# Value projections as pairs of chunks of 512 output columns by half the contraction

## The reference

```
layer 0:  x += 0.5 ffn(x);  x += pool_mixer(x) + memory_attention;  x += 0.5 ffn(x)
layer 1:  x += 0.5 ffn(x);  x += diff_attention(x) + memory_attention;  x += 0.5 ffn(x)
layer 2:  x += norm(moba(x), retention(x));  x += norm(cross_attention(x, mem));  x += norm(ffn(x))

memory values, layers 0 and 1:  v = mem_n @ mem_w_kv[:, 512:1024]       256 x 512
differential attention:         v = h @ w_in[:, 2048:3072]              256 x 1024, 8 heads of 128
layer 2:                        mv = h @ w_in[:, 1024:1536]             256 x 512, 8 heads of 64
                                rv = h @ w_in[:, 2048:2560]             256 x 512, 4 heads of 128
cross attention:                v = mem_n @ w_ckv[:, 1024:2048]         256 x 1024
```

## Time and profile before

| | |
|---|---|
| median of three executions | 1621.92 us |
| profiled execution, first to last instruction | 1619.9 us |
| matmuls busy | 1520.8 us, 94% |
| VectorE busy | 1033.5 us, 64% |
| ScalarE busy | 722.8 us, 45% |
| mean granted TensorE clock | 0.976 |
| weights and inputs read | 254.64 MB, 158 GB/s |

### The profile page before, as it was taken

One profiled execution on the slowest core, in us unless ns is written; L12 is line 12 of the kernel. 1 busy time (PEld: TensorE's weight loads), 2 busy tenths in 40 slices (PEclk: granted clock), 3 DMA queues, 4 the chain that ended last, 5 costly groups with the idle time before them and its releaser, 6 DMA issues.

```text
span 1619.9 us, 28718 instructions
## 1 busy us (share of the span) xinstructions
PE 1520.8 (94%) x12056; PEld 1483.4 (92%) x12056; DVE 1033.5 (64%) x1234; ACT 722.8 (45%) x905; POOL 1.9 (0%) x7
## 2 busy tenths in 40 slices
PE   5999998999999999999989999999898999799996
PEld 5999998999999999999977999999787898699996
DVE  5555588665455755568777864557857864764555
ACT  5443454454344544454445544445344443343442
POOL 0000000000000000000000000000000000000000
PEclk9999999999999999999989999999999899799998
DMA  6655553445555445544333345454334242245450
GB/s 240 222 179 186 182 182 104 157 147 180 193 177 179 165 180 181 187 177 172 114 105 118 143 160 204 167 180 173 118 117 156 88 173 105 104 141 198 173 181 35
DMA packets 35837, 256.84 MB, mean 159 GB/s; under 512 B 3984, under 2 KB 4112, under 8 KB 4912
## 3 DMA queue, kind: packets, MB, share of 16 engines
q1 hardware_dynamic: 35424, 253.48, 44.0%
q0 software_dynamic: 336, 2.23, 0.3%
HBM read 254.64 MB, written 1.05 MB: 158 GB/s over the span
## 4 chain that ended last, share of the span: by engine, by line
PE 80%; DVE 14%; ACT 4%; issue 1%; DMA 0%; SPq 0%; ACTq 0%; DVEq 0%
PE prod L791 16%; PE prod L792 16%; PE prod L793 16%; PE acc L791 8%; PE acc L793 8%; PE acc L792 8%; DVE four L1253 4%; DVE w_lo L1206 3%; ACT w_hi L1018 1%; DVE acts_l L1258 1%; PE prod L820 1%; PE prod L822 1%; PE prod L821 1%; PE aux L843 1%; PE acc L896 1%
## 5 line engine op out<-in xcount | busy, mean ns | idle before, releaser
L791 PE MATMUL prod<-acts_h,w_hi 128*128 128x256 f32 x2352 | 679.2, 289 | 35.7 <-DVE w_lo L1206 18.2
L792 PE MATMUL prod<-acts_l,w_hi 128*128 128x256 f32 x2352 | 672.3, 286 | 0.0
L793 PE MATMUL prod<-acts_h,w_lo 128*128 128x256 f32 x2352 | 671.9, 286 | 0.0
L1206 DVE TENSOR_TENSOR w_lo<-raw,w_hi 128x2048 fp32r<-128x2048 f32 x238 | 543.8, 2286 | 57.2 <-ACT w_hi L1018 57.0
L1018 ACT CAST w_hi<-raw 128x2048 fp32r<-128x2048 f32 x238 | 451.5, 1899 | 166.7 <-PE acc L793 102.8
L791 PEld LDWEIGHTS prod<-acts_h,w_hi 128*128 128x128 f32 x2352 | 458.1, 195 | 40.0 <-DVE w_lo L1206 18.2
L792 PEld LDWEIGHTS prod<-acts_l,w_hi 128*128 128x128 f32 x2352 | 458.1, 195 | 1.2 <-issue 1.0
L793 PEld LDWEIGHTS prod<-acts_h,w_lo 128*128 128x128 f32 x2352 | 457.7, 195 | 0.0
L791 PE MATMUL acc<-mix_h,w_hi 128*128 128x256 f32 x1200 | 343.2, 286 | 3.2 <-DVE mix_l L1524 2.2
L792 PE MATMUL acc<-mix_l,w_hi 128*128 128x256 f32 x1200 | 340.6, 284 | 0.0
L793 PE MATMUL acc<-mix_h,w_lo 128*128 128x256 f32 x1200 | 340.5, 284 | 0.0
(11 more groups left out here) (152 smaller groups left out, 961.8 us busy)
## 6 DMA issues: line engine op xcount, KB each, us to landing
raw<-in_weights_dram SPq DMA_DIRECT2D x238, 1024.0 KB, 4.8
mem_x<-in_mem_dram POOLq DMA_DIRECT2D x2, 1024.0 KB, 6.6
tabs<-in_tabs_dram SPq DMA_DIRECT2D x1, 1697.0 KB, 13.2
x_res<-in_x_dram SPq DMA_DIRECT2D x2, 512.0 KB, 6.3
out_dram<-x_res SPq DMA_DIRECT2D x4, 256.0 KB, 2.1
masked<-in_lambda_dram POOLq DMA_DIRECT2D x1, 128.0 KB, 3.0
vecs<-in_vecs_dram SPq DMA_DIRECT2D x1, 64.5 KB, 1.8
```

The lines of the kernel that those rows point to most:

```text
L791: pe.matmul(out, w(w_hi, slot), moving_hi, start=first, stop=False, skip_group_check=True)
L792: pe.matmul(out, w(w_hi, slot), moving_lo, start=False, stop=False, skip_group_check=True)
L793: return pe.matmul(out, w(w_lo, slot), moving_hi, start=False, stop=last, skip_group_check=True)
L1206: dve.tensor_tensor(w_lo[:, c % RING], raw[:, c % RAW], w_hi[:, c % RING].bitcast(F32), ALU.subtract).then_inc(lo_done, 1)
```

## The change

Each pair of token chunks now covers 512 output columns, each chunk by half of the contraction. `project_tokens` adds two items, and a matmul streams 512 columns into a whole product bank: tokens 0 to 127 in one bank, tokens 128 to 255 in the other. Both banks are started in the first chunk and finished in the second. VectorE reads both after the second chunk, one operation of 128x512 for each.

In the differential mixer the order is now q0 k0 q1 v01 k1 q2 k2 q3 k3 v23. In layer 2's mixer the two chunks of mv are together, where the first one was, and the two of rv as before; what stood between such chunks now stands behind the pair.

```diff
+    def project_tokens(self, source, col, dest, at):
+
+        for k_half in range(2):
+            self.weights()
+            self.chunks.append((*source, "half", (k_half, col)))
+            self.add("rows_half", c=self.c, e=self.e, k_half=k_half, dest=dest, at=at, acts=self.acts)
+            self.c += 1
+            self.acts_users = self.c
+        self.e += 2
...
-        for n in range(2):
-            pl.project(("mem_w_kv", layer), 512 + n * COLS, "mem_v", n * COLS, tokens_out=True)
+        pl.project_tokens(("mem_w_kv", layer), 512, "mem_v", 0)
...
-    for name, pair in (("q", 0), ("k", 0), ("q", 1), ("v", 0), ("k", 1), ("q", 2), ("k", 2), ("v", 1),
-                       ("q", 3), ("k", 3), ("v", 2), ("v", 3)):
-        col = {"q": 0, "k": D, "v": 2 * D}[name] + pair * COLS
+    for name, pair in (("q", 0), ("k", 0), ("q", 1), ("v", 0), ("k", 1), ("q", 2), ("k", 2),
+                       ("q", 3), ("k", 3), ("v", 2)):
...
-            pl.project(w, col, "v", pair * COLS, tokens_out=True)
-            pl.ready_v(mine)
+            pl.project_tokens(w, 2 * D + pair * COLS, "v", pair * COLS)
+            pl.ready_v(heads[2 * pair:2 * pair + 4])
...
-        if pair < 3 or name != "v":
+        for _ in range(2 if name == "v" and not pair else 1):
             interleave(ticks, 2)
             norms.step()
...
-    pl.project(w, 1024, "v", 0, tokens_out=True)
-    pl.ready_v(moba[0:4])
+    pl.project_tokens(w, 1024, "v", 0)
+    pl.ready_v(moba)
     pl.rope("k", 6, "ret", pl.e - 1)
     pl.ready(ret)
     interleave(ticks, 2)
-    for n in range(2):
-        pl.project(w, 2048 + n * COLS, "v", 512 + n * COLS, tokens_out=True)
-        if n:
-            pl.ready_v(ret)
-        interleave(ticks, 2)
+    pl.project_tokens(w, 2048, "v", 512)
+    pl.ready_v(ret)
+    interleave(ticks, 4)
...
     norms.step()
-    pl.project(w, 1024 + COLS, "v", COLS, tokens_out=True)
-    pl.ready_v(moba[4:8])
     pl.rope("k", 2, "moba", pl.e - 1)
...
-    for n in range(4):
-        pl.project(("w_ckv_2", 0), D + n * COLS, "mem_v", n * COLS, tokens_out=True)
+    for n in range(2):
+        pl.project_tokens(("w_ckv_2", 0), D + 512 * n, "mem_v", 512 * n)
...
+            def tokens_half(it):
+
+                slot, k_half = it["c"] % RING, it["k_half"]
...
                 for t in range(2):
+                    e = it["e"] + t
+                    if k_half == 0 and e >= 2:
+                        pe.wait_ge(prod_read, e - 1)
+                    out = prod[e % 2][:].rearrange("p a b -> p (a b)")
+                    for n in range(4):
+                        kt = 4 * k_half + n
                         a_h = acts_h[:, kt, t * P:(t + 1) * P]
                         a_l = acts_l[:, kt, t * P:(t + 1) * P]
+                        wh = w_hi[:, slot, n * 512:(n + 1) * 512]
+                        wl = w_lo[:, slot, n * 512:(n + 1) * 512]
                         pe.matmul(out, a_h, wh, start=(kt == 0), stop=False, skip_group_check=True)
                         pe.matmul(out, a_h, wl, start=False, stop=False, skip_group_check=True)
                         mm = pe.matmul(out, a_l, wh, start=False, stop=(kt == KT - 1), skip_group_check=True)
+                mm.then_inc(chunk_used, 1)
...
-                    elif kind == "rows_out":
+                    elif kind == "rows_half" and it["k_half"]:
                         e = it["e"]
                         dve.wait_ge(chunk_used, c + 1)
                         for t in range(2):
-                            ins = dve.tensor_scalar(tok_dests[it["dest"]][:, t, it["at"]:it["at"] + COLS],
-                                                    prod[e % 2][:, t], rstd[:, 0, S + t:S + t + 1], None, ALU.mult)
-                        ins.then_inc(prod_read, 1)
+                            dve.tensor_scalar(tok_dests[it["dest"]][:, t, it["at"]:it["at"] + 512],
+                                              prod[(e + t) % 2][:].rearrange("p a b -> p (a b)"),
+                                              rstd[:, 0, S + t:S + t + 1], None, ALU.mult).then_inc(prod_read, 1)
```

More of the change, by code:

```diff
@@ L150, in chunk @@
         self.c += 1
-        if kind in ("cols", "rows_out"):
+        if kind == "cols":
             self.acts_users = self.c
@@ L217, in ffn, with project @@
         return item
-    def project(self, source, col, dest, at, tokens_out=False, **k):
-        return self.chunk("rows_out" if tokens_out else "cols", (*source, "cols", col), dest=dest,
-                          at=at, acts=self.acts, **k)
+    def project(self, source, col, dest, at):
+        return self.chunk("cols", (*source, "cols", col), dest=dest, at=at, acts=self.acts)
+    def project_tokens(self, source, col, dest, at):
[6 more added lines that the diff above has]
+        self.e += 2
     def ticks(self, units):
@@ L583, in lay_out_chunk @@
         out.reshape(P, KT, COLS)[...] = v
+    elif how == "half":
+        k_half, col = at
+        v = w.reshape(2, 4, P, -1)[k_half][:, :, col:col + 512].transpose(1, 0, 2)
+        out.reshape(P, 4, 512)[...] = v
     elif how == "rows":
@@ L806, in columns_chunk @@
                 return mm
-            def tokens_chunk(slot, bank, acts):
-                if seen["acts"] < acts:
-                    pe.wait_ge(acts_lo, acts)
-                    seen["acts"] = acts
-                for t in range(2):
-                    for kt in range(KT):
+            def tokens_half(it):
+                slot, k_half = it["c"] % RING, it["k_half"]
+                if seen["acts"] < it["acts"]:
+                    pe.wait_ge(acts_lo, it["acts"])
+                    seen["acts"] = it["acts"]
+                for t in range(2):
+                    e = it["e"] + t
[4 more added lines that the diff above has]
+                        kt = 4 * k_half + n
                         a_h = acts_h[:, kt, t * P:(t + 1) * P]
                         a_l = acts_l[:, kt, t * P:(t + 1) * P]
-                        wh = w_hi[:, slot, kt * COLS:(kt + 1) * COLS]
-                        wl = w_lo[:, slot, kt * COLS:(kt + 1) * COLS]
-                        out = prod[bank][:, t]
+                        wh = w_hi[:, slot, n * 512:(n + 1) * 512]
+                        wl = w_lo[:, slot, n * 512:(n + 1) * 512]
                         pe.matmul(out, a_h, wh, start=(kt == 0), stop=False, skip_group_check=True)
@@ L822, in tokens_chunk @@
                         mm = pe.matmul(out, a_l, wh, start=False, stop=(kt == KT - 1), skip_group_check=True)
-                return mm
+                mm.then_inc(chunk_used, 1)
             def down_chunk(slot, tiles, first, last):
@@ L954, in _ @@
                         ffn_part(it, p, 0)
-                elif kind in ("cols", "rows_out", "down", "group"):
+                elif kind in ("cols", "rows_half", "down", "group"):
                     c = it["c"]
@@ L959, in _ @@
                         reader(pe, told)
-                    if kind in ("cols", "rows_out"):
+                    if kind == "cols":
                         if it["e"] >= 2:
                             pe.wait_ge(prod_read, it["e"] - 1)
-                        part = columns_chunk if kind == "cols" else tokens_chunk
-                        part(c % RING, it["e"] % 2, it["acts"]).then_inc(chunk_used, 1)
+                        columns_chunk(c % RING, it["e"] % 2, it["acts"]).then_inc(chunk_used, 1)
+                    elif kind == "rows_half":
+                        tokens_half(it)
                     elif kind == "down":
@@ L1608, in number @@
         it["late_readers"] = []
-        if kind in ("cols", "rows_out", "group", "ffn"):
+        if kind in ("cols", "rows_half", "group", "ffn"):
             it["late_readers"], late_readers = late_readers, []
```

2 lines of the change are left out of this document (1 added, 1 removed).

## The result

The kernel after takes 1638.33 us (median of 4 runs, 1637.16 to 1638.61), the kernel before 1621.59 (4 runs) beside it: ratio 1.0091, 95% interval 1.0071 to 1.0110. It is slower by 0.9%, 7 us more than forecast and inside the range.

A forecast was written before the change was run, and what follows sets the result against it. TensorE, busy 94% of the 1619.9 us span, was taken as the bound. Stage terms -2.3 - 1.4 + 0.4 + 5.8 = +2.5 us and +6.3 for the clock gave 1628.7 us of span, forecast as 1631 us, range 1615 to 1641.

The forecast's parts named there:

- saving per chunk: All 16 value chunks: 24 matmuls at 0.2155 us take 5.17 us instead of 5.76, 0.59 us less each.
- memory values, both: Memory values of both layers: shorter matmuls less 0.1 us given back, -2.3 us.
- cross values: Cross stage: four chunks 0.59 us shorter each, less one 0.95 us bank wait between its pairs, -1.4 us.
- second mixer: Differential mixer, 794 to 918 us: new waits against a removed 7.0 us wait and shorter matmuls, +0.4 us.
- third mixer: Layer 2's mixer, 1154 to 1256 us: +7.7 us up to the k chunk's end, then -1.9, sum +5.8 us.
- clock: Half clock behind new idle stretches: three falls of 2.1 us counted, +6.3 us; none +0, all five +10.5.
- the rival in which the pitch grows with the columns: Value matmuls: 0.24 us each at 512 columns, +9.4 us on the forecast, 1640 us; chance 0.07.
- if the pitch is not near 0.216 us: Sign of a wrong forecast: the 512-column value matmuls not starting about 0.216 us apart.
- The bank waits: Between the cross pairs and at the third mixer's rotary matmul: 0.95 us each; nothing more at other memory and cross exits.
- saving carries: Rival: waits added at heads 2, 4, 6 don't come, k2 transpose waits under 1 us; 1609 to 1614.4 us; chance 0.10.
- the idle stretches that the prediction gave as signs: 2 to 4 us on the last pair's value read; 4 to 6 us before the second k rotary matmul and in the drain.
- the five thin stretches: TensorE thin at 808 to 813, 867 to 876, 884 to 890, 1181 to 1190, 1214 to 1218 us; three falls counted.

The follow-up runs named there:

- e1: Kernel before plus a tail of unread fast float32 matmuls of four widths; pitch 0.228, 0.174, 0.119, 0.110 us at 512, 384, 256, 128 columns.
- e6_early: Kernel after, but VectorE reads each pair's first bank while TensorE still fills the second: 1632.7 us, 1.0052 of the kernel before.
- e11_fill_head2: Kernel before with 56 unread matmuls in the 7.4 us gap ahead of head 2's V matmul: 1623.1 us, ratio 0.9987.
- e8: Kernel after with unread matmuls put into three TensorE gaps, two in the second mixer and one in the third: 1636.8 us, 1.0073 of the kernel before.
- e12: Kernel before with pairs only for memory and cross values, early read of each pair's first bank, 56 unread matmuls before head 2's V matmul: 1621.4 us, ratio 0.9984.
- e5: Kernel after; third mixer only: two ticks between halves of each value pair, second gate chunk between the rotary steps: 1638.8 us, 1.0085 of the kernel before.
- e2_order_only: Kernel after's order, but every value chunk in its old 256-column form: 1636.5 us, 1.0078 of the kernel before.
- e10: Kernel before with 56 unread matmuls ahead of head 0's V matmul, where no gap is: 1630.9 us, ratio 1.0043.
- e3_unmoved: Kernel before with wide pairs only for memory values and the cross stage, both mixers unchanged: 1622.4 us, ratio 0.9990.

## Why the prediction was right, and where not

Sign, class and range were right; the size was 7 us short. The range was 26 us wide, so its holding says little for the steps. By these, in the profiled executions (16.2 us of span, where 8.8 were forecast; the measured stretches add up to 1.4 us more than that, since the last part of the program, which nothing changed, came out 1.6 us shorter):

| step | forecast | measured |
|---|---|---|
| saving per chunk | 0.59 | 0.31 |
| memory values, both | -2.3 | +0.1 |
| cross values | -1.4 | +1.45 |
| second mixer | +0.4, clock apart | +1.8, clock apart; +3.7 in all |
| third mixer | +5.8, clock apart | +4.9, clock apart; +12.3 in all |
| clock | +6.3 | about 9 in the mixers (1.9 + 7.4) |

"Clock apart" is the change of idle time less the 1.2 us that the four chunks save.

- The first failed step is the pitch. From the uneven start in the earlier trace rows I read the 0.013 us as a weight load that a longer stream would hide, and took L843's full-precision matmul as the nearest row. The fast matmul has 0.013 to 0.015 us beside its columns at 384 and 512 columns as well (e1), where L843's 0.2155 leaves 0.002 beside twice 0.107. That is 4.5 us of the miss, and the rival in which the pitch grows with the columns (0.24) was about as near as my 0.2155. The earlier trace rows held the alternative: 0.12 at full clock, 0.213 at half. It should have been an end of the range of its own, "one fixed time per matmul", at -5 us. By its own sign ("if the pitch is not near 0.216 us") the prediction counts this as a miss: 0.011 us is 5% of the pitch, but half of the saving. The Trainium skill ("TensorE: Matmul & The Clock Gate", "Back-to-back issue gap") states a sustained 131 ns for 512 columns; this matmul does not show it, its pitch is 0.227 us.
- The bank waits came as mechanism and nearly as size: 0.9 us of wait (gap 1.33) between the cross pairs and 0.8 (gap 1.23) at the rotary step, for 0.95. What was costed at nothing was not: at the exits of the memory and cross pairs the two long reads stand ahead of the `acts_l` work on VectorE, and the gap there is 2.38 us for 1.73; e6_early, which takes that away, shortens a memory stage by 0.6 us.
- The second mixer's waits were forecast behind the first pair as 1.5 + 2.8 (gaps of 1.67 and 2.94), at head 2 as 2.2 (3.89), at the last pair as 3.7 (1.49), in the drain as 5.8 (1.94 + 3.97). So the rival "saving carries" fell at its own test, the transpose behind the k2 chunk. The wrong ones offset each other partly; that the sum came within 1.4 us of the forecast is luck in part. Idle time rose by 3.0 us though the 7.0 us wait was gone. Of the idle stretches that the prediction gave as signs, the drain's longest gap, 3.97 us, is just under the 4 to 6, and the last pair's value read cost 1.1 us for 2 to 4.
- In the third mixer the gate chunk came 9.2 us late, counted from the first value chunk (1191.6, for 1190.05 forecast; 1182.39 before), the rotary wait was 4.8 for 4.7. Idle time rose by 6.1 us; less the 1.2 saved that is 4.9 for the forecast 5.8, in which 2.4 of saving were counted. So the waits were forecast at 8.2 and measured 6.1.
- The clock was the right mechanism and under-counted. I counted 3 falls of 2.1 us. Busy time rose by 0.7 and 6.2 us in the mixers, in each of which four chunks saved 0.31 each (1.2), which makes 1.9 + 7.4 = 9.3 us, as an estimate. Length times the missing clock gives the same order: in the third mixer 142.49 x 0.10 = 14.2 against 130.19 x 0.05 = 6.5. Half clock stood behind four of the five thin stretches that the prediction listed, from 811.1, 886.2, 1193.4 and 1234.3 us, and at places it did not list, 841.8 and 920.3 us among them. The 3 us too little here and the 4.5 of the pitch nearly make up the 7.4 of the miss. The Trainium skill ("TensorE: Matmul & The Clock Gate", "Why this matters for your kernels") says that idle gaps between bursts of matmuls bring the clock down. e11_fill_head2 agrees: with its gap filled, the clock stayed at 1.00. But which gap brings a fall I could not tell from it: in e8 and e12 the falls moved.

## What to carry to other kernels

Before pricing a wider matmul, split the pitch you have into columns and a rest by two widths or two clock levels, and keep the whole rest. Merging two chunks of work takes away a place where a waiting chain had cover; write down for every chain which chunk covers it before and after, since a wait that is removed comes up at the next uncovered chain (e5), and price its idle time by its length and, as a second term, by the clock behind it: in e2_order_only, with the matmuls of the kernel before, the second term was 6.2 us and the first 8.0. Where a wait cannot be shortened, work that nobody needs can keep the clock up (e11), if it is shorter than the wait and stands exactly there (e10). Here that was worth 3.6 us in one execution and 0.13% over all.

## What the hardware showed beyond that

- A fast float32 matmul of 128 columns takes 0.110 us, nearly as long as one of 256 (0.119): going from 256 to 128 columns gains next to nothing.
- Shifting a stage by a few us, or its gaps, changed where the half clock fell in stages whose code was the same: 1.8 us in the third mixer of e12_combined, 1.2 us ahead of the third mixer's first value chunk in the kernel after.
- A gap of 2.38 us at the exit of the memory values was followed by 3.4 us at half clock, one of 1.73 us was not (kernel after against kernel before; e3_unmoved and e6_early agree). But one of 2.46 us, at 917.71 us of the kernel before, was not either, so these rows give no limit.
